# Order of loads and squares in the first stage of a two-block transformer kernel

## What is computed

```
mod   = silu(c) @ w_ada + b_ada;  shift, scale, gate = split(mod, 3)
h     = rms_norm(x, g_pre) * (1 + scale) + shift          # block 1
mem_h = rms_norm(mem, mem_norm_g)                         # block 2, 256 rows
k, v  = split(mem_h @ w_mem_kv, 2);  k = rms_norm(k per head of 256)
```

## Time and profile before

| | us |
|---|---|
| median of 3 runs | 1152.31 (1152.17 to 1152.65) |
| the profiled execution | 1153.57 |
| its span in the trace | 1151.8 |
| TensorE matmul busy | 1124.1 (98%) |
| TensorE weight loads busy | 919.5 (80%) |
| VectorE busy | 819.5 (71%) |
| ScalarE busy | 585.8 (51%) |
| GpSimd busy | 66.2 (6%) |

### The profile page before, as it was taken

The page is one execution under the profiler, slowest core; times in us unless marked ns, Lnnn a source line. Parts: engine busy times, 40 slices in busy tenths (PEclk is TensorE's granted clock), DMA queues, the critical chain, the costliest instruction groups (busy, mean ns, idle before and its releaser), DMA issues.

```text
span 1151.8 us, 15721 instructions
## 1 busy us (share of the span) xinstructions
PE 1124.1 (98%) x5796; PEld 919.5 (80%) x5796; DVE 819.5 (71%) x1424; ACT 585.8 (51%) x1084; POOL 66.2 (6%) x73
## 2 busy tenths in 40 slices
PE   5899999999999999999999999999999999999998
PEld 5898777766898877877778778888888888788887
DVE  5788655668566347999999985898777787853342
ACT  6663555456565455766766663325553223651230
POOL 2019500101000000000000000000000000000000
PEclk9899999999999999999999999999999999999999
DMA  9967422321355322212222242323223333223221
GB/s 343 353 218 256 128 72 74 92 65 38 129 169 197 109 75 73 74 38 92 74 92 74 72 145 96 110 77 106 74 74 98 123 98 104 92 73 110 93 72 73
DMA packets 35276, 130.20 MB, mean 113 GB/s; under 512 B 4272, under 2 KB 4656, under 8 KB 34688
## 3 DMA queue, kind: packets, MB, share of 16 engines
q1 hardware_dynamic: 31536, 112.74, 29.3%
q0 software_dynamic: 3376, 16.23, 4.2%
q10 hardware_dynamic: 288, 0.24, 0.1%
HBM read 121.59 MB, written 6.29 MB: 111 GB/s over the span
## 4 chain that ended last, share of the span: by engine, by line
PE 89%; DVE 5%; ACT 3%; DMA 2%; issue 2%; SPq 0%; POOL 0%; DVEq 0%; ACTq 0%
PE bank L475 27%; PE bank L477 26%; PE bank L476 26%; PE bank L726 2%; PE bank L577 2%; DMA raw<-in_chunks 2%; PE bank L847 2%; PE bank L754 1%; DVE wl L1813 1%; PE bank L680 1%; ACT qf L1211 1%; DVE stat L1969 0%; DVE cumt L2502 0%; ACT wh L1130 0%; PE bank L716 0%
## 5 line engine op out<-in xcount | busy, mean ns | idle before, releaser
L475 PE MATMUL bank<-hl,wh 128*128 128x512 f32 x888 | 357.9, 403 | 0.0
L477 PE MATMUL bank<-hh,wh 128*128 128x512 f32 x888 | 347.0, 391 | 0.0
L476 PE MATMUL bank<-hh,wl 128*128 128x512 f32 x888 | 346.2, 390 | 0.0
L1813 DVE TENSOR_TENSOR wl<-raw,wh 128x1024 fp32r<-128x1024 f32 x185 | 225.1, 1238 | 103.8 <-ACT wh L1130 103.0
L1130 ACT ACTIVATE wh<-raw 128x1024 fp32r<-128x1024 f32 x185 | 192.0, 1058 | 205.8 <-PE bank L477 186.3
L475 PEld LDWEIGHTS bank<-hl,wh 128*128 128x128 f32 x888 | 167.1, 188 | 36.6 <-issue 3.1
L477 PEld LDWEIGHTS bank<-hh,wh 128*128 128x128 f32 x888 | 166.7, 188 | 36.2
L476 PEld LDWEIGHTS bank<-hh,wl 128*128 128x128 f32 x888 | 167.2, 188 | 31.3 <-issue 0.7
L2225 DVE SCALAR_TENSOR_TENSOR ca<-u,vt,ca 128x512 f32<-128x512 f32 x232 | 157.9, 746 | 0.0
L476 PE MATMUL bank<-oh,wl 128*128 128x512 f32 (+1 forms) x256 | 94.0, 367 | 0.0
L477 PE MATMUL bank<-oh,wh 128*128 128x512 f32 (+1 forms) x256 | 93.9, 367 | 0.0
(11 more groups left out here) (337 smaller groups left out, 1649.1 us busy)
## 6 DMA issues: line engine op xcount, KB each, us to landing
raw<-in_chunks SPq DMA_DIRECT2D x193, 512.0 KB, 3.6
ada_a<-in_chunks SPq DMA_DIRECT2D x8, 512.0 KB, 11.6
ada_b<-in_chunks SPq DMA_DIRECT2D x8, 512.0 KB, 9.5
x<-in_x POOLq DMA_DIRECT2D x4, 512.0 KB, 10.5
mem_scratch<-kvm POOLq DMA_DIRECT2D x1, 2048.0 KB, 9.5
x<-in_x POOLq DMA_DIRECT2D x1, 2048.0 KB, 8.5
x_scratch<-x POOLq DMA_DIRECT2D x1, 2048.0 KB, 7.7
kvm<-mem_scratch POOLq DMA_DIRECT2D x1, 2048.0 KB, 9.3
```

The costliest lines, as they stand in the source:

```text
L475: pe.matmul(o, a[0], b[1], start=start, stop=False, **kw)
L476: pe.matmul(o, a[1], b[0], start=False, stop=False, **kw)
L477: return pe.matmul(o, a[0], b[0], start=False, stop=stop, **kw)
L1813: dve.tensor_tensor(wl[:, w], raw[:, RAW_SLOT[nxt]], wh[:, w].bitcast(F32), ALU.subtract)\
```

## The change

- SP waits for both tiles of the memory before it issues mk1. Each of the first 16 `ada` pieces is issued only after an earlier load has landed: pieces 0 to 2 after mk1 to mk3, piece n after piece n - 3.
- `ADA_BEHIND` moves the first pieces later: mk2 and mk3 now come before ada0.
- GpSimd waits for the memory before it issues `x` and all that follows.
- The squares of the memory's second tile are made on VectorE, into a scratch row of `macc`.
- Before the memory's copies only mk0 is split, no longer mk1 too.
- ScalarE's squares of x move behind `ahead` of head 0 (tiles 0 and 1) and of head 1 (tiles 2 and 3, then the root). VectorE's `xn` moves from h == 0 to h == 2.
- The counts of squares that later waits use fall by one, from 6 to 5.

```
-ADA_BEHIND = (0, 2, 1, 2, 1, 1, 1, 1, 1, 1, 1, 1, 2, 1, 0, 0, 0, 2, 0, 2, 0, 2, 0, 2)
+ADA_BEHIND = (0, 0, 0, 2, 1, 2, 1, 2, 1, 2, 1, 2, 1, 1, 0, 0, 0, 2, 0, 2, 0, 2, 0, 2)
...
+                if name == ("mk", 1):
+                    sp.wait_ge(s.mem_in, 16 * 2)
+                if name[0] == "ada" and name[1] < ADA_EARLY:
+                    wait_raw(sp, ("ada", name[1] - 3) if name[1] > 2 else ("mk", name[1] + 1))
                 sp.dma_start(raw_rows(name), t["chunks"][STORED.index(("wo" if name[0] == "wp" else name[0], name[1]))])\
...
         def _(pool):
+            pool.wait_ge(s.mem_in, 16 * 2)
             for tt in range(T):
...
-        squared_at = {name: 6 + 2 * n + 2 for n, name in enumerate(SQUARED)}
+        squared_at = {name: 5 + 2 * n + 2 for n, name in enumerate(SQUARED)}
...
             act.wait_ge(s.mem_in, 16 * 2)
-            square_rows(memx, MEM_SS, 2)
-            act.wait_ge(s.sumsq, 2)
+            square_rows(memx, MEM_SS, 1)
+            act.wait_ge(s.sumsq, 1)
+            act.wait_ge(s.mem_squared, 1)
             act.activation(MEM_SS, MEM_SS, ACT.Sqrt, scale=1.0 / D, bias=eps6).then_inc(s.small_sqrt, 1)
             act.wait_ge(s.rows_in, 16)
             act.activation(tc_, v8("c"), ACT.Tanh, scale=0.5).then_inc(s.c_tanh, 1)
-            ahead(None, 2)
+            ahead(None, 1)
...
             ahead(None)
-            act.wait_ge(s.x_in, 16 * T)
-            square_rows(x, X_SS, T)
-            act.wait_ge(s.sumsq, 6)
-            act.activation(X_SS, X_SS, ACT.Sqrt, scale=1.0 / D, bias=eps6).then_inc(s.small_sqrt, 1)
...
                 ahead(("mk", 2 * h + 1))
+                if h < 2:
+                    act.wait_ge(s.x_in, 16 * T)
+                    square_rows(x[:, 2 * h:2 * h + 2], X_SS[:, 2 * h:2 * h + 2], 2)
+                if h == 1:
+                    act.wait_ge(s.sumsq, 5)
+                    act.activation(X_SS, X_SS, ACT.Sqrt, scale=1.0 / D, bias=eps6).then_inc(s.small_sqrt, 1)
...
-                    if squares[0] > 6:
+                    if squares[0] > 5:
...
             dve.memset(eps5, 1e-5).then_inc(s.eps_done, 1)
+            dve.wait_ge(s.mem_in, 16 * 2)
+            dve.tensor_tensor_reduce(macc[:, 0, :], memx[:, 1, :], memx[:, 1, :], 1.0, 0.0, ALU.mult, ALU.add,
+                                     MEM_SS[:, 1:2]).then_inc(s.mem_squared, 1)
...
-            ahead(None, 2)
+            ahead(None, 1)
...
                 ahead(("mk", 2 * h + 1))
-                if h == 0:
+                if h == 2:
                     dve.wait_ge(s.small_sqrt, 2)
                     then(dve.reciprocal(X_SS, X_SS))
```

More of the change, by code:

```diff
@@ L149 @@
     "tables_in": "masks, distances and blocks loaded",
-    "mem_in": "memory loaded", "x_in": "x loaded", "bcast_in": "lambdas and sinks loaded on every partition", "late_in": "positions, gate bias and gain",
+    "mem_in": "memory loaded", "mem_squared": "squares of the memory's second tile added up", "x_in": "x loaded", "bcast_in": "lambdas and sinks loaded on every partition", "late_in": "positions, gate bias and gain",
     "swapped": "halves of heads swapped for the rotation", "wmask_in": "banded masks of two tiles loaded", "sel_in": "rows that pick a head's bias loaded",
```

## The result

The changed kernel takes 1157.76 us (median of 5, 1156.89 to 1160.39) against 1152.17 us (median of 5 on the same chip): the ratio is 1.0053, with a 95% interval from 1.0038 to 1.0067. It is slower by about 5.6 us, and that is clear of the 0.2% bound. The profiled execution took 1157.50 us with a span of 1155.6, 3.8 more than the span of before.

A forecast was written before the change was run, and what follows sets the result against it. TensorE, busy 1124.1 of 1151.8 us, was taken as the bound, so order gains only where it idles or runs slowly. Transposes 2.0 later plus 2.5 for the clock gave +4.5, 1156.8 us; own range 1154.6 to 1159.0, overall 1152.5 to 1159.9.

The forecast's parts named there:

- The start: Before the old hole: memory lands 1.0 us sooner, first transpose 9.6 for 11.13, mk1 to mk3 without a hole to 25.2.
- mk5's landing: Eleventh transfer on SP's queue, issued by 16.6, lands at 26.5, bounds 23.1 and 27.6.
- ScalarE's chain: From mk5's landing through x's squares and root to mv0's high: 15.6 us, so 42.1.
- VectorE's order: From 42.1, two lows, three pieces, reciprocal and four tiles take 8.9 us; `xn` complete at 51.0.
- TensorE: Waits about 2.2 for mk6's low, then idles 41.7 to 51.1 for `xn`, 9.4 us; transposes 2.0 later than before.
- the term: Clock at 0.50 after the new hole: 2.5 us lost, now behind the 49.12 mark.
- the hole before: TensorE's hole from 28.4 to 33.3 in the kernel before; called half idle and the rest thin, it would vanish.
- clock kept: Rival: transposes 2.0 late but the clock doesn't fall or recovers at once; +2.0, 1154.3; chance 0.09.
- Fast landing: Rival: mk5 lands at 23.1, `xn` at 47.6; -1.5 and +2.5 for the clock, +1.0, 1153.3; chance 0.09.
- Faster: Rival: `xn` complete before TensorE asks at 41.7, net gain 7.4, 1144.9; chance 0.12.
- Queue dry: Rival: landings SP waits for let the engines run empty, mk5 at 29.5; +7.6, 1159.9; chance 0.07.
- The gap that the prediction allowed for behind the memory: Transfers after the memory: only mk0 feeds the engines for 1.25 us while new issues need 2.35; up to 1.1.

The follow-up runs named there:

- 7: The first experiment's kernel with the start undone: x and mk1 not held, memory squared on ScalarE, mk1 split before the memory's copies; 1147.41 us, ratio 0.9960.
- the first experiment: Changed kernel with `xn` written ahead of the `ahead` call (mv0, ada8, mv1, ada9, ada10) on VectorE in h == 2; 1149.46 us, ratio 0.9979.
- the fourth experiment: Changed kernel with 72 unread 128x256 matmuls added on TensorE ahead of its wait for `xn`; 1155.97 us, ratio 1.0031.
- sixth: The first experiment's kernel with 16 unread 128x256 matmuls added on TensorE ahead of the first value matmuls; 1148.58 us, ratio 0.9967.
- eleventh: The same code as 7 (`xn` first, start undone), measured once more; 1150.27 us, ratio 0.9978.
- second: Changed kernel with x's squares, their root and `xn` put back where they stood before; loads stay changed; 1151.43 us, ratio 0.9989.
- third: Kernel before with only the move of x's squares and of `xn` to h == 2; 1161.55 us, ratio 1.0076.
- eighth: The first experiment's kernel without the waits that keep three `w_ada` pieces in flight; 1150.53 us, ratio 0.9977.
- ninth: 7 plus 16 unread 128x256 matmuls ahead of the first value matmuls; 1150.04 us, ratio 0.9971.
- the tenth: Kernel before with only x's squares moved and `xn` written ahead of the `ahead` call in h == 2; 1154.42 us, ratio 1.0015.

## Why the prediction was right

The forecast was 1156.8 and +4.5 us; measured were 1157.76 and +5.6, with an interval from 4.4 to 7.7 us.

- **The start.** First transpose 9.75 for 9.6. The parts were less exact: the memory landed 0.4 us sooner, not 1.0 (6.25 for 6.67), and VectorE's multiply-and-add of the second tile took 1.22 us for 1.3. mk1 to mk3 ran without a hole to 25.56, for 25.2. That this start would be absorbed followed from mk5's landing, and 7 shows it.
- **mk5's landing.** 16.75 plus 8.8 is 25.55, for 26.5 and bounds of 23.1 and 27.6. Issue and landing in the views of SP's queue and of the DMA issues:

```profile
16.75 0.33 SPq L1019 DMA_DIRECT2D raw<-in_chunks  x1
```

```profile
raw<-in_chunks SPq DMA_DIRECT2D x1, 512.0 KB, 8.8
```

- **ScalarE's chain.** mv0's high was over at about 42.1, as forecast. Here two errors cancelled: mk5 came 0.9 early, and a wait that I had not priced, 0.92 us for mk7 at 33.49, gave it back, which was luck. The table loads followed one another as in the rows, 1.28 us and the next operation 1.29 later (36.80 to 38.09). So the drain that the Trainium skill counts (ScalarE: Activation LUTs, What ACT_TABLE_LOAD costs) does not show in this spacing either.
- **VectorE's order.** `xn` complete at 51.01, for 51.0. The step that decides is this one, and the first experiment shows it: the same instructions in the other order give `xn` at 41.75 (39.01 plus 2.74) and a median 8.3 us lower.
- **TensorE.** Hole of 9.2 us, for 9.4; transposes at 51.06, for 51.1; then 5.1 us at 0.50, which cost 2.43, for 2.5. The fourth experiment shows the term: 2.36 us less with the clock kept up. TensorE waited 0.86 for mk6's low, not 2.2, and then 0.69 for the third head's squares (40.72), a wait that the sum did not have; so it reached the hole at 41.85, for 41.7, with two errors against each other.
- **What was mis-sized.** The prediction calls the hole before half idle; its own row has 1.12 us of work in 4.90. It also says that nothing takes the loss up, and 0.6 us came back. The traces show 3.8 us between the two spans where the sum had 4.5; that the median says 5.6 comes in part from which runs stand on the other side, as said above. And the sum took the slow stretch behind the one-column block as fixed. In the profiled execution it was (3.4 us, 73.4 to 76.8), but from run to run it is not, and a part of the 5.6 may be that. The traces of single executions don't settle the last microsecond.

Of the rivals, clock kept is refuted by the stretch at 0.50. Fast landing came nearest in its cause: mk5 was early by 0.9 of the 3.4 us that this rival asked for, and it was of no use. Faster described a real kernel, but another one: with `xn` ahead of the call it is complete at about 41.8, and the time is 0.2 to 0.4% below before. Its 7.4 us were out of reach even so, because TensorE then waits 2.00 us for mv1's low, a wait that this rival left out. Queue dry did not occur: from 9 to 25 us, while mk5 was on its way, the DMA share was 1.03. The gap that the prediction allowed for behind the memory was there, but small: 0.81 and 254 GB/s from 7 to 9 us, against 1.03 and 420 before.

## What to carry to other kernels

When work moves to a later place in one engine's program, price the place, not the work: list every instruction that now stands in front of it on the engine that makes it and on the one that feeds it, and find the landing that the first of them waits for. Here the edit closed a hole of 3.8 us of idle time and opened one of 9.2, because four cheap scalings stood behind a chunk whose high part ScalarE made only after everything else. And a gain ahead of the next landing on the path is no gain: the start was 1.4 us earlier, and the seventh experiment, without it, was no slower.

## What the runs showed of the hardware beyond that

After the block of one-column matmuls TensorE's clock falls to its lower level, 0.50, and for how long varied. In the profiled executions it was about 3.4 us in four kernels (before, changed, sixth, eleventh) and about 6.8 us in six (first, second, third, seventh, eighth, ninth). The same code gave both: 6.8 us in one execution (first row, the seventh experiment) and 3.4 in another (second row, the eleventh, 0.79 on average over 8 us):

```profile
64.00:71.00 7.00, 7.00 (x37) 7.00 (x37) 6.89 (x18) 3.56 (x6) 0.00 (x0) 0.57 0.72 283
```

```profile
63.00:71.00 8.00, 8.00 (x56) 8.00 (x56) 7.89 (x19) 4.20 (x7) 0.00 (x0) 0.79 0.63 246
```

In the fourth and the tenth it did not fall behind the same block at all, and `fa` came that much earlier: from the second transposes to `fa` it took 22.58 and 22.59 us there, 24.06 before and 24.07 in the eleventh, 25.63 in the seventh. So such a stretch costs between nothing and 3 us.

How much of the spread between runs it explains is open. Each timed run has a mean granted clock on record, though not the place where it was low. Within one kernel the slower runs are mostly those with the lower clock: in the tenth experiment 1151.12 and 1151.23 us at 1.000 and 0.999, and 1156.54 to 1157.74 at 0.994; in the eighth 1148.29 to 1148.65 at 0.999 to 1.000, and 1151.20 to 1153.36 at 0.995 to 0.997. But it is not all: four runs of the eleventh, all at 0.999, took 1147.40 to 1150.27. And the seventh and the eleventh, one code, differ by 1.8 us in the mean (2.9 in the median), while their clocks, 0.9986 and 0.9980 on average, make about 0.7 us of it (0.0006 of 1150, an estimate). What decides the length of the stretch was not tested.
